# Attention outputs folded into the second half of their own PSUM bank, reciprocals one unit ahead, keys of two heads in one product

## What is computed

```python
q = (rms_norm(c_q, q_norm_g) @ w_uq).reshape(B, S, 8, 64 + 32)
q_nope, q_rope = q[..., :64], rope(q[..., 64:], cos, sin)
kv = (rms_norm(c_kv, kv_norm_g) @ w_ukv).reshape(B, S, 8, 64 + 64)
k_nope, v = kv[..., :64], kv[..., 64:]
k_rope = rope(k_r, cos, sin)                     # one for all heads
s = (q_nope @ k_nope.T + q_rope @ k_rope.T) * 96 ** -0.5
mask = key // 64 <= query // 64                  # causal by chunks of 64
p = softmax(where(mask, s, -inf))
out = p @ v                                      # per head, 64 columns
```

## Time and profile before

| what | us |
|---|---|
| median of three runs (lowest, highest) | 2718.45 (2716.57, 2719.48) |
| the profiled execution | 2722.13 |
| its span, first to last instruction | 2720.3 |
| mean granted TensorE clock, share of full speed | 0.957 |
| TensorE busy with products (share of the span) | 2411.5 (89%) |
| VectorE busy | 1557.7 (57%) |
| ScalarE busy | 1157.7 (43%) |
| GpSimd busy | 317.3 (12%) |

### The profile page before, as it was taken

How to read it: one execution, slowest core, us unless ns; L and a number is a source line. 1 busy time by engine, 2 the same in 40 slices (tenths; PEclk the granted TensorE clock), 3 DMA queues, 4 the chain that set the end, 5 groups by cost and what they waited for, 6 DMA issues and landing times. The chain is left out here.

```text
span 2720.3 us, 39975 instructions
## 1 busy us (share of the span) xinstructions
PE 2411.5 (89%) x12168; PEld 1804.8 (66%) x12169; DVE 1557.7 (57%) x2674; ACT 1157.7 (43%) x1903; POOL 317.3 (12%) x221
## 2 busy tenths in 40 slices
PE   5999999999799998999996999369999999999960
PEld 3776776766456566565664788258777788888840
DVE  3323444323476676776774444648787865656638
ACT  2222223122355565555663221046665644545433
POOL 0000000000000000000000111012333322222215
PEclk9999999999799999999997999589999999999985
DMA  5000000000000000000004322479999988878836
GB/s 208 16 24 8 23 23 15 23 8 8 22 7 5 8 13 6 9 12 6 9 6 143 118 93 93 145 287 359 309 376 312 334 292 278 268 229 276 291 69 247
DMA packets 148675, 338.23 MB, mean 124 GB/s; under 512 B 24672, under 2 KB 36576, under 8 KB 148320
## 3 DMA queue, kind: packets, MB, share of 16 engines
q1 hardware_dynamic: 135488, 289.45, 29.1%
q0 software_dynamic: 13104, 47.72, 7.2%
HBM read 288.38 MB, written 57.67 MB: 127 GB/s over the span
## 5 line engine op out<-in xcount | busy, mean ns | idle before, releaser
L1763 DVE TENSOR_TENSOR w_raw<-w_raw,w_hi 128x4096 f32 (+1 forms) x96 | 424.6, 4423 | 145.4 <-ACT w_hi L1754 145.4
L1754 ACT CAST w_hi<-w_raw 128x4096 fp32r (+1 forms) x96 | 347.7, 3634 | 122.3 <-DMA w_raw<-in_w 111.5
L1703 PE MATMUL eH<-w_hi,xh 128*128 128x512 f32 x720 | 290.6, 404 | 17.3 <-DVE xl L1821 17.3
L1704 PE MATMUL eH<-w_hi,xl 128*128 128x512 f32 x720 | 286.8, 398 | 0.0
L954 ACT CAST prT_hi<-pT 128x512 fp32r<-128x512 f32 (+1 forms) x288 | 162.1, 563 | 268.1 <-PE pT L871 268.0
L853 PE MATMUL pS<-kT,qT 128*128 128x512 f32 (+3 forms) x640 | 259.8, 534 | 5.4 <-ACT pr L946 4.9
L1023 DVE TENSOR_TENSOR prT_lo<-pT,prT_hi 128x512 fp32r<-128x512 f32 (+1 forms) x288 | 189.3, 659 | 123.6 <-ACT prT_hi L954 122.5
L1281 POOL TENSOR_TENSOR hp<-hp,b 128x1024 f32<-128x1024 f32 x16 | 40.7, 2546 | 1633.2 <-DVE hp L1336 1633.2
L1014 DVE TENSOR_REDUCE mx<-pS 128x1 f32<-128x512 f32 (+2 forms) x320 | 194.5, 610 | 24.4 <-PE pS L853 17.4
L1708 PE MATMUL eH<-w_raw,xh 128*128 x720 | 184.6, 398 | 4.2 <-DVE w_raw L1763 4.2
L853 PEld LDWEIGHTS pS<-kT,qT 128*128 128x128 f32 x640 | 111.0, 190 | 107.9 <-issue 72.5
(11 more groups left out here) (291 smaller groups left out, 4242.0 us busy)
## 6 DMA issues: line engine op xcount, KB each, us to landing
w_raw<-in_w SPq DMA_DIRECT2D x96, 2048.0 KB
xt<-in_x SPq DMA_DIRECT2D x8, 1024.0 KB, 4.8
wi<-in_w_in SPq DMA_DIRECT2D x4, 2048.0 KB, 17.7
xs<-in_x SPq DMA_DIRECT2D x8, 1024.0 KB, 4.9
scratch_h<-hp SPq DMA_DIRECT2D x16, 512.0 KB, 3.0
fz<-scratch_z SPq DMA_DIRECT2D x16, 512.0 KB, 9.6
out<-fz SPq DMA_DIRECT2D x16, 512.0 KB, 2.6
scratch_rT<-ot SPq DMA_DIRECT2D x8, 512.0 KB, 2.9
```

The source lines that it names most:

```text
L1703: pe.matmul(H[:], xh[:, k, :], w.hi[:, k, :], start=(k == 0), stop=False)
L1704: pe.matmul(H[:], xl[:, k, :], w.hi[:, k, :], start=False, stop=False)
L1754: nc.scalar.copy(w.hi[:], w.words(o).bitcast(F32)).then_inc(w.hi_ready, 1)
L1763: v.tensor_tensor(w.words(o), w.words(o).bitcast(F32), w.hi[:].bitcast(F32), ALU.subtract).then_inc(w.lo_ready, 1)
```

## The change

Four edits, all in `phase_b` and its tables.

1. The fold no longer takes a pT bank. It writes columns 256 to 383 of the pO bank that its step was weighed into, and `divide` reads them there. Units alone rotate over the pT banks. `FOLD_LAG` goes from 2 to 1. The first weighing of step n + 2 waits for `divide(n)`.
2. The sum of row sums and its reciprocal (`invert`) are issued on VectorE one slot earlier than the division.
3. Keys of two heads are projected in one product with 128 output rows, for even heads only, so 16 in place of 32. The second head's keys lie in rows 64 to 127, and for odd heads the halves of kT and qT are swapped. kT gets four tiles in place of two; the rope rows of the two new ones are copied by GpSimd (`rope_again`).
4. The folding matrix becomes a constant of its own (`stack`) with a DMA of its own at the program's start; the opening rope product fills all 128 rows.

```diff
-    fold[:64, 64:] = (s[:64, None] % 32 == s[None, :64] % 32)
-    fold[:, :64] = (s[:, None] % 64 == s[None, :64])
+    fold[:64] = (s[:64, None] % 32 == s[None, :] % 32)
     c["fold"] = fold
+    c["stack"] = (s[:, None] % VD == s[None, :VD]).astype(np.float32)
...
-                sp.wait_ge(loaded, 160)
+                sp.wait_ge(loaded, 176)
...
-LAG, RING, FOLD_LAG = 4, 6, 2
+LAG, RING, FOLD_LAG = 4, 6, 1
...
-    return [(kind, h, c) for c in range(4) for kind in (("k", "q", "v") if h % 2 == 0 else ("k", "q"))]
+    return [(kind, h, c) for c in range(4) for kind in (("k", "q", "v") if h % 2 == 0 else ("q",))]
...
-T_ORDER = [e for s in range(SLOTS + 1) for e in ([("unit", s)] if s < NU else []) + ([("fold", FOLD_SLOT[s])] if s in FOLD_SLOT else [])]
-T_AT = {e: n for n, e in enumerate(T_ORDER)}
...
-        kT = sb("kT", [P, 2, SEQ])
+        kT = sb("kT", [P, 4, SEQ])
...
-        O = [psum(f"pO{i}")[:, 0:2 * P] for i in range(2)]
+        O = [psum(f"pO{i}") for i in range(2)]
...
-                        ins = pe.matmul(b[0:64, :], wk[:, g, x, :], t["ckvn"][:, at], start=True, stop=True)
+                        ins = pe.matmul(b[:], wk[:, g], t["ckvn"][:, at], start=True, stop=True)
...
                     pe.wait_ge(exp_done, EXP_AT[n][1] + g // 2 + 1)
-                    b = free_turn(T_AT["unit", u])
+                    if u >= NTB:
+                        pe.wait_ge(t_lo, u - NTB + 1)
+                    b = T[u % NTB]
...
                     if g == 0 and n >= 2:
-                        pe.wait_ge(o_copied, n - 1)
+                        pe.wait_ge(a_ready, n - 1)
...
                     pe.wait_ge(o_copied, n + 1)
-                    b = free_turn(T_AT["fold", n])
                     for i in range(2):
-                        ins = pe.matmul(b[:, i * VD:(i + 1) * VD], oT[:, n % 2, i * P:(i + 1) * P], t["fold"][:, 0:VD], start=True, stop=True)
+                        ins = pe.matmul(O[n % 2][:, 2 * P + i * VD:2 * P + (i + 1) * VD], oT[:, n % 2, i * P:(i + 1) * P], t["stack"][:],
+                                        start=True, stop=True)
...
-                        nc.scalar.copy(kT[0:64, h % 2, at], b[0:64, :]).then_inc(k_copied, 1)
+                        for x in range(2):
+                            half = slice(x * 64, x * 64 + 64)
+                            nc.scalar.copy(kT[half, (h + x) % 4, at], b[half, :]).then_inc(k_copied, 1)
...
+            @block.gpsimd
+            def _(pool):
+
+                pool.wait_ge(rope_copied, 8)
+                for x in range(2):
+                    half = slice(64 - 64 * x, 128 - 64 * x)
+                    nc.gpsimd.tensor_copy(kT[half, 2 + x], kT[half, x]).then_inc(rope_again, 1)
...
-                def divide(n):
-                    h, q = STEPS_B[n]
+                def invert(n):
                     both = slice(2 * n, 2 * n + 2)
                     v.wait_ge(exp_done, EXP_AT[n][1] + PIECES[n][1])
                     v.tensor_reduce(rin[:, both], rsum[:, both], AX, ALU.add).then_inc(rs_ready, 1)
                     v.wait_ge(rs_ready, n + 1)
                     v.reciprocal(rin[:, both], rin[:, both]).then_inc(rin_ready, 1)
+
+                def divide(n):
...
                             if s < NU:
                                 rest(s)
+                            if s in COPY_SLOT:
+                                invert(COPY_SLOT[s])
                             if s in FOLD_SLOT:
                                 divide(FOLD_SLOT[s])
```

More of the change, by code:

```diff
@@ L144, in lay_out @@
     w = a["w_uq"][0].reshape(Q_RANK, HEADS, NOPE + ROPE)
-    w = w[:, :, np.concatenate([np.arange(96), np.arange(80, 96), np.arange(64, 80)])]
+    even = np.concatenate([np.arange(96), np.arange(80, 96), np.arange(64, 80)])
+    w = np.stack([w[:, h, np.roll(even, h % 2 * 64)] for h in range(HEADS)], axis=1)
     a["w_uq"] = np.ascontiguousarray(w.reshape(Q_RANK, HEADS // 2, 2, P).transpose(1, 0, 2, 3))
@@ L173, in _ @@
                 for dst, src in (
-                    (t["ident"][:], d["ident"]), (t["causal"][:], d["causal"]), (t["fold"][:], d["fold"]),
+                    (t["ident"][:], d["ident"]), (t["causal"][:], d["causal"]), (t["fold"][:], d["fold"]), (t["stack"][:], d["stack"]),
                     (t["cols"][:], d["cols"]), (t["restart"][:], d["restart"]),
@@ L202, in step @@
                     v.wait_ge(steps, n[0])
-                v.wait_ge(loaded, 160)
+                v.wait_ge(loaded, 176)
                 step(v.tensor_copy(ang[:], pos_i[:]))
@@ L685 @@
 V_AT = [sum(2 * (p[0] == "v") for p in PREP[:n]) for n in range(len(PREP) + 1)]
-K_AT = [sum(p[0] == "k" for p in PREP[:n]) for n in range(len(PREP) + 1)]
+K_AT = [sum(2 * (p[0] == "k") for p in PREP[:n]) for n in range(len(PREP) + 1)]
 Q_AT = [sum(p[0] == "q" for p in PREP[:n]) for n in range(len(PREP) + 1)]
@@ L802, in _ @@
                 for c in range(4):
-                    ins = pe.matmul(S[c][64:128, :], t["fold"][0:64, 64:128], t["krp"][0:64, c * 512:(c + 1) * 512],
-                                    start=True, stop=True, tile_position=(0, 64))
+                    ins = pe.matmul(S[c][:], t["fold"][0:64, :], t["krp"][0:64, c * 512:(c + 1) * 512], start=True, stop=True)
                     ins.then_inc(folded, 1)
@@ L846, in score @@
                     if i == 0:
-                        pe.wait_ge(k_copied, 4 * h + q // 2 + 1)
+                        if h == 2:
+                            pe.wait_ge(rope_again, 2)
+                        pe.wait_ge(k_copied, K_AT[PREP_NO["k", h - x, q // 2] + 1])
                         pe.wait_ge(q_copied, 4 * h + q // 2 + 1)
@@ L852, in score @@
                         keys = slice(j * 512, j * 512 + w)
[L853 to L863, removed]
+                        pe.matmul(b[:, 0:w], qT[:, x, at], kT[:, h % 4, keys], start=True, stop=True).then_inc(scored, 1)
                 def turn(u):
@@ L921, in _ @@
                     for x in range(2):
-                        nc.scalar.copy(kT[64:128, x, c * 512:(c + 1) * 512], S[c][64:128, :]).then_inc(rope_copied, 1)
+                        half = slice(64 - 64 * x, 128 - 64 * x)
+                        nc.scalar.copy(kT[half, x, c * 512:(c + 1) * 512], S[c][half, :]).then_inc(rope_copied, 1)
                 def copy(p):
@@ L929, in copy @@
                     if kind == "q":
-                        nc.scalar.copy(qT[0:64, h % 2, at], b[0:64, :]).then_inc(q_copied, 1)
+                        half = slice(h % 2 * 64, h % 2 * 64 + 64)
+                        nc.scalar.copy(qT[half, h % 2, at], b[half, :]).then_inc(q_copied, 1)
                     elif kind == "k":
-                        nc.scalar.copy(kT[0:64, h % 2, at], b[0:64, :]).then_inc(k_copied, 1)
+                        for x in range(2):
+                            half = slice(x * 64, x * 64 + 64)
+                            nc.scalar.copy(kT[half, (h + x) % 4, at], b[half, :]).then_inc(k_copied, 1)
                     else:
@@ L953, in cast @@
                     w = len(pair_halves(*UNITS[u])) * P
-                    nc.scalar.copy(ph[:, u % RING, 0:w], T[T_AT["unit", u] % NTB][:, 0:w]).then_inc(t_hi, 1)
+                    nc.scalar.copy(ph[:, u % RING, 0:w], T[u % NTB][:, 0:w]).then_inc(t_hi, 1)
                 def copy_o(n):
@@ L959, in copy_o @@
                         act.wait_ge(o_folded, n - 1)
-                    nc.scalar.copy(oT[:, n % 2], O[n % 2]).then_inc(o_copied, 1)
+                    nc.scalar.copy(oT[:, n % 2], O[n % 2][:, 0:2 * P]).then_inc(o_copied, 1)
                 for p in prep_of(0):
@@ L987, in rope @@
                     v.wait_ge(prep, m + 1)
-                    v.tensor_tensor(qT[64:128, h % 2, at], S[S_AT["prep", p] % 4][64:128, :], t["trig"][64:128, at], ALU.mult).then_inc(q_roped, 1)
+                    half = slice(64 - h % 2 * 64, 128 - h % 2 * 64)
+                    v.tensor_tensor(qT[half, h % 2, at], S[S_AT["prep", p] % 4][half, :], t["trig"][half, at], ALU.mult).then_inc(q_roped, 1)
                 def split_v(p):
@@ L1022, in rest @@
                     v.wait_ge(t_hi, u + 1)
-                    v.tensor_tensor(pl[:, u % RING, 0:w], T[T_AT["unit", u] % NTB][:, 0:w], ph[:, u % RING, 0:w].bitcast(F32),
+                    v.tensor_tensor(pl[:, u % RING, 0:w], T[u % NTB][:, 0:w], ph[:, u % RING, 0:w].bitcast(F32),
                                     ALU.subtract).then_inc(t_lo, 1)
-                def divide(n):
-                    h, q = STEPS_B[n]
+                def invert(n):
                     both = slice(2 * n, 2 * n + 2)
@@ L1036, in divide @@
                         v.wait_ge(a_stored[n % 4], 16 * (n // 4))
-                    v.tensor_tensor(a[:, n % 4], T[T_AT["fold", n] % NTB][:, 0:2 * VD].rearrange("p (i c) -> p i c", i=2),
+                    v.tensor_tensor(a[:, n % 4], O[n % 2][:, 2 * P:2 * P + 2 * VD].rearrange("p (i c) -> p i c", i=2),
```

(1 more changed line is left out.)

11 lines of the change are left out of this document (6 added, 5 removed).

## The result

The changed kernel takes 2656.6 us (median of 4 runs, 2656.5 to 2658.64), the kernel before 2718.97 us (2716.57 to 2725.64): a ratio of 0.9769, 95% interval 0.9751 to 0.9786, so 62 us saved. I had predicted 2672.5 us with a range of 2656 to 2697. The direction and the cause were right.

The account below looks back on a forecast made before the run. TensorE bounds the attention stage, waiting at turns and folds for VectorE's splits. -41 - 11.5 + 1 + 2 + 3 + 0.5 = -46 us takes the median of 2718.45 to 2672.5 us, range 2656 to 2697.

Parts of the forecast that it names:

- term A: Attention stage: removing TensorE's waits at turns and folds for VectorE's splits gains 41 us, bounds 22 to 47.
- Direct loss: TensorE's waits at folds and turns behind them, including unrecorded time: 27.5 + 8.3 + 10.9 = 46.7 us.
- the two waits that the new fold brings: Folds late behind their copy, +2 us; first weighings of step n+2 waiting for the division, +3 us.
- The walk through the halves: Placing operations one by one in half-steps holding a fold: 11.8 us gained for two heads, 47 for eight.
- I take off 0.3 us in each of five such halves: Halves with three pieces: VectorE has little slack, so some 6 us of the gain is taken off.
- term B: Key projections, 32 to 16, in the small steps of heads 0, 2, 4 and 6: 11.5 us gained, bounds 6 to 16.
- The 30% taken off for VectorE: Small steps of even heads: VectorE is near its limit, so only 70% of the keys' 16.0 us is taken.
- one costs what it did: A key product with 128 output rows and the same 512 columns takes as long as one with 64.
- the copies by ScalarE: Two key copies of 0.57 us in a row can delay a cast in 16 steps: +1 us, bounds 0 and 9.
- VectorE's queue: Rival: VectorE's queue takes over, leaving a gain of 27 us, so 2691 us; chance 0.18.
- The O bank's longer hold: Rival: copy, fold and division in series on one bank become the bottleneck, +37 us, 2756 us; chance 0.04.
- The turns' waits: Rival: these don't go, as cast and split behind two banks hold TensorE; about -5 us, 2713 us; chance 0.04.

Follow-up runs that it names:

- The fold alone: The kernel before with the fold's own bank, earlier slot and earlier reciprocals, key projections per head as before: ratio 0.9829, 46.5 us saved.
- late reciprocals: The changed kernel with the row sums' reduction and reciprocal back in front of the division, behind the split: 2662.45 us, ratio 0.9794.
- an added maximum: The changed kernel with one more unused maximum of a piece on VectorE in each half of three pieces: ratio 0.9806.
- the keys alone: The kernel before with one key product for two heads, the fold still in the pT rotation: ratio 0.9932, 18.5 us saved.

## Why the prediction held, and where it was too low

**The bottleneck and the waits (term A): right in kind, 11 us too small with its costs.** Direct loss 46.7 us, forecast 41 after 6 us taken off for VectorE, and 36 after the 2 and 3 us for the two waits that the new fold brings. The fold alone, with all that belongs to it, gave 46.5 us in time and 47.1 in the stretch. The walk through the halves was the good instrument: it said 47 us before the discount. The half of the earlier trace rows became 0.92 us shorter where I had 0.94; the halves with the fold last 1.03 and 1.05 where I had 0.93; those with three slots and the fold in the middle 1.41 in two places and 1.01 in the third (even heads, q of 5, first half) where I had 1.3. What failed is the step "I take off 0.3 us in each of five such halves". Of the kinds of halves that the prediction gives a number for, it came true in that third place alone, the half that late reciprocals lengthened by 0.30 us and an added maximum by 1.20. Elsewhere VectorE started its work earlier along with TensorE, since its splits wait for casts that wait for turns: its wait for casts fell from 122.5 us to 93.5. The slack that I read in a trace with stalls (0.28 us of wait in the earlier trace rows) was not the slack that there is without them.

**The keys (term B): mis-sized, 18.3 against 11.5.** Two things. The 30% taken off for VectorE was wrong: with the keys alone, the small steps of even heads gave 16.5 us, all of the 16.0. (Not evenly: at q of 0 in heads 2, 4 and 6 nothing was gained, elsewhere mostly 1.1 to 1.2 us for a removed projection, as the scores ahead of it end sooner too.) And "one costs what it did" was wrong in my favour: a product with 128 rows takes 0.14 us less than one with 64, and the product ahead of it 0.09 less, so the 16 that are left in odd heads and at the opening are faster too (2.4 us in the small steps of odd heads). With the earlier trace rows alone this couldn't be seen, since every key projection of the kernel before was narrow; the queries' projections beside it, 128 rows and the same columns, would have shown it.

**What I had missed: the parts overlap.** 6.6 us are lost between them, where my sum had 1 us for the copies by ScalarE; the copies are at least 2.2 of it, nearly all in odd heads (2.1). The 2.3 us lost in the small steps of even heads I put down to the missing filler, since moving the queries there gives back more than that (5.9). Some 2 us stay without an experiment. The exponential "ended at 918.50, before the projection began" was right for the kernel before; once both parts had shortened the step, the same exponential ended after the scores, at 899.38 against a turn possible near 898.

**The waits that the change adds** were smaller than taken: weighings wait 1.8 us for the division (I had 3), and no wait of a product behind `copy_o` is in the list (I had 2). The load of the new constant, 0.5 us, can't be told from the 4 us by which the stage's start varies among the profiles (710.7 to 714.8). The two copies by GpSimd took 3.83 us in all from 719.12 us (I had up to 5 each), nothing waits for them, and VectorE's splits in the opening took 0.76 us for two, as before. The reciprocals, counted at nothing, are worth 2.8 us in the profile.

**The wait for a bank** that the Trainium skill's rule calls for (PSUM — Partial Sum Buffer, "PSUM bank collisions raise a hardware error") is there and costs 1.8 us, in 3 places of the 6 that the code allows. What would happen without it no run shows. Two engines do read one bank at once elsewhere, but in different partitions: behind a query projection VectorE takes rows 64 to 127 from 918.19 for 0.69 us and ScalarE rows 0 to 63 from 918.49 for 0.57 us (kernel before), and nothing in the code keeps them apart.

**The rivals.** VectorE's queue did not take over (2691 us): the stretch is 58.8 us shorter, where this rival allowed the 33.5 us that VectorE had waited for TensorE. It was given 0.18 and, worse, both discounts came from it, which made the forecast a mixture of two cases rather than the likeliest one. The O bank's longer hold did not bind (1.8 us of waits, and none behind a copy). The turns' waits went: the 10.5 us left are near the 8.6 that had never stood behind a fold.

**The sum and the range.** Added up in the stretch: 47.1 for the fold (forecast 36), 18.3 for the keys (11.5), 6.6 lost between them (1), together 58.8. The forecast had 46 in all, with 0.5 for the new constant, so it was 18 us too low in the two parts, and the loss that it had too small took back nearly 6 of them. The range's fast end was added up wrongly: "47 and 16 gained, costs as taken" is 2718.45 - 63 + 6.5 = 2662 us; 2656 is what comes out with no costs at all. Against the end that my own terms give, the measured 2656.6 us lies outside. That it falls inside the range as stated is luck.

## What to carry to other kernels

A small product that takes a turn in a rotation of buffers costs the wait of its neighbours, not its own time: 64 folds of 0.45 us, 29 us in all, sat beside 47 us of waits. Look for room that is already owned by the same work (the unused half of its bank) before adding a buffer. When a part is shortened everywhere, move the remaining filler to where the removed one had stood: moving the query projections by a small change brought 6.6 us in the stretch. And don't discount a gain by the idle time that the second engine shows in a trace with stalls; place the next few operations one by one instead, and look at each kind of half by itself: the discount was right in one and wrong in the others.

## What the hardware showed that I had not expected

A product of 512 columns with 64 output rows holds TensorE for 1.00 us where one with 128 rows holds it for 0.86 (two passes each, at a granted clock of 1.00), and doing the useless half made a kernel 5 us faster in the stretch (ratio 0.9980, 0.9967 to 0.9994). The product ahead pays 0.09 us more, too. Of the 0.24 us in all, 0.19 lie at the two edges between a product of 128 rows and one of 64, where the load of weights doesn't start ahead of its product; between the two passes of the narrow product, where the width stays, it does (918.78 for the pass at 919.21), and 0.05 us are lost. This points at the change of width rather than at the width, but no run has narrow products side by side, so the two aren't told apart.
